# Where the moving operands of split matmuls start in on-chip memory: from 160, 352 and 448 modulo 512 bytes to 64

## The reference

```python
# first block
xn = rms_norm(x, attn_norm_g); proj = xn @ w_in            # 1024 x 3088
y  = concat(moba_attention(...), gated_linear_attention(...) * silu(gr))
x  = x + y @ w_out
hn = rms_norm(x, ffn_norm_g)
h  = causal_dwconv(hn @ w_ffn_up); x = x + (silu(h_gate) * h_val) @ w_ffn_down   # D_FF 2816
x  = rms_norm(x, final_norm_g)
# second block; shifts, scales and gates come from silu(c) @ w_ada + b_ada
x = x + 0.5 * g1 * swiglu(modulate(rmsnorm(x), sh1, sc1), ffn1_w_in, ffn1_w_out)
z = modulate(rmsnorm(x), sh2, sc2) @ w_in_2
y_a = mla_attention(...) @ w_branch_a; y_b = chunk_attention(...) @ w_branch_b
x = x + g2 * ((sigmoid(gate_a) * y_a + sigmoid(gate_b) * y_b) @ w_out_2)
x = x + 0.5 * g3 * swiglu(modulate(rmsnorm(x), sh3, sc3), ffn2_w_in, ffn2_w_out)
return rmsnorm(x, final_norm)
```

## Time and profile before

| | us |
|---|---|
| median of 3 runs | 947.26 |
| lowest, highest | 946.65, 947.27 |
| the profiled execution | 948.89 |
| its span, first to last instruction | 947.2 |
| PE busy in it | 913.0 |
| DVE busy | 698.1 |
| ACT busy | 461.8 |

### The profile page before, as it was taken

How to read it: one execution, slowest core, us unless ns; L and a number is a source line. 1 busy time by engine, 2 the same in 40 slices (tenths; PEclk the granted TensorE clock), 3 DMA queues, 4 the chain that set the end, 5 groups by cost and what they waited for, 6 DMA issues and landing times.

```text
span 947.2 us, 19952 instructions
## 1 busy us (share of the span) xinstructions
PE 913.0 (96%) x7412; PEld 873.5 (92%) x7412; DVE 698.1 (74%) x1080; ACT 461.8 (49%) x698; POOL 64.9 (7%) x109
## 2 busy tenths in 40 slices
PE   7999999999999999999998989999999999999996
PEld 5989898999999988999998979888899899999995
DVE  6498866988889958988889877667757665566444
ACT  4655555755553436433342445656544643444332
POOL 1021101000002210100002121000000000000000
PEclk9999999999999999999999999999999999999998
DMA  7443346556658973988879945543455265655641
GB/s 248 134 143 126 113 144 212 178 179 194 187 193 323 409 287 115 341 286 276 282 253 347 410 175 171 167 153 116 130 173 190 86 201 195 191 186 178 213 142 45
DMA packets 53325, 191.57 MB, mean 202 GB/s; under 512 B 5921, under 2 KB 6433, under 8 KB 53153
## 3 DMA queue, kind: packets, MB, share of 16 engines
q1 hardware_dynamic: 41760, 149.96, 47.2%
q0 software_dynamic: 10656, 39.33, 11.4%
q10 hardware_dynamic: 864, 1.67, 0.5%
HBM read 189.89 MB, written 1.05 MB: 202 GB/s over the span
## 4 chain that ended last, share of the span: by engine, by line
PE 81%; DVE 10%; DMA 4%; ACT 2%; issue 2%; DVEq 0%; ACTq 0%; SPq 0%; POOLq 0%
PE ps L325 24%; PE ps L326 23%; PE ps L327 23%; DMA raw<-w 3%; DVE w_lo L1074 2%; PE ps L399 2%; DVE rstd L1079 1%; PE ps L388 1%; PE ps L389 1%; PE ps L390 1%; DVE ada_raw L1332 1%; PE ps L414 1%; PE ps L471 1%; ACT w_hi L752 1%; PE ps L445 1%
## 5 line engine op out<-in xcount | busy, mean ns | idle before, releaser
L325 PE MATMUL ps<-xh,w_hi 128*128 128x256 f32 x1472 | 416.5, 283 | 11.8 <-DVE xl L1100 10.0
L326 PE MATMUL ps<-xl,w_hi 128*128 128x256 f32 x1472 | 412.8, 280 | 0.0
L327 PE MATMUL ps<-xh,w_lo 128*128 128x256 f32 x1472 | 412.3, 280 | 0.0
L1074 DVE TENSOR_TENSOR w_lo<-raw,w_hi 128x1024 fp32r<-128x1024 f32 x282 | 339.9, 1225 | 97.3 <-ACT w_hi L752 96.9
L752 ACT ACTIVATE w_hi<-raw 128x1024 fp32r<-128x1024 f32 x282 | 288.8, 1056 | 132.6 <-PE ps L327 72.8
L325 PEld LDWEIGHTS ps<-xh,w_hi 128*128 128x128 f32 x1472 | 278.1, 189 | 18.4 <-issue 10.4
L326 PEld LDWEIGHTS ps<-xl,w_hi 128*128 128x128 f32 x1472 | 278.2, 189 | 0.4 <-issue 0.2
L327 PEld LDWEIGHTS ps<-xh,w_lo 128*128 128x128 f32 x1472 | 278.2, 189 | 0.0
L325 PE MATMUL ps<-act_hi,w_hi 128*128 (+1 forms) x528 | 150.4, 285 | 6.1 <-DVE w_lo L1074 6.1
L326 PE MATMUL ps<-act_lo,w_hi 128*128 (+1 forms) x528 | 149.0, 282 | 0.0
L327 PE MATMUL ps<-act_hi,w_lo 128*128 (+1 forms) x528 | 148.9, 282 | 0.0
(11 more groups left out here) (237 smaller groups left out, 926.4 us busy)
## 6 DMA issues: line engine op xcount, KB each, us to landing
raw<-w SPq DMA_DIRECT2D x282, 512.0 KB, 4.3
ada_raw<-ada_w POOLq DMA_DIRECT2D x72, 512.0 KB, 7.2
X<-x_in SPq DMA_DIRECT2D x4, 256.0 KB, 6.5
bm<-bias_in POOLq DMA_DIRECT2D x1, 1024.0 KB, 5.1
out<-X SPq DMA_DIRECT2D x4, 256.0 KB, 2.1
tab<-tab_in ACTq DMA_DIRECT2D x1, 640.0 KB, 9.1
gmask<-gmask_in ACTq DMA_DIRECT2D x1, 512.0 KB, 11.1
cact<-c_in POOLq DMA_DIRECT2D x1, 512.0 KB, 4.8
```

Source lines behind the costliest of these rows:

```text
L325: pe.matmul(o, lh, rh, start=start, stop=False, skip_group_check=True)
L326: pe.matmul(o, lh, rl, start=False, stop=False, skip_group_check=True)
L327: return pe.matmul(o, ll, rh, start=False, stop=stop, skip_group_check=True)
L1074: v.tensor_tensor(w_lo[:, slot(h), :], raw[:, slot(h), :], w_hi[:, slot(h), :].bitcast(F32), ALU.subtract).then_inc(lo_ready, 1)
```

## The change

Three pads change. `off_line`, ahead of xh and xl, grows from 32 to 448 bytes. `on_line`, behind them, grows from 32 to 352 bytes. A new tensor `line2` of 416 bytes stands in the second block's set, between st2 and bm; nothing reads or writes it.

```diff
-        sb("off_line", [P, 8])
+        sb("off_line", [P, 112])
         xh = sb("xh", [P, KC, S], F32R)
         xl = sb("xl", [P, KC, S], F32R)
-        sb("on_line", [P, 8])
+        sb("on_line", [P, 88])
...
-                    ("sm2", [P, 2, 768], F32), ("pt2", [P, 2, 768], F32), ("st2", [P, 2, 3, 4], F32),
+                    ("sm2", [P, 2, 768], F32), ("pt2", [P, 2, 768], F32), ("st2", [P, 2, 3, 4], F32), ("line2", [P, 104], F32),
                     ("bm", [P, 8, S], F32), ("th", [P, 16, S], F32)],
                    early=[("lat", [P, 3, S], F32), ("latsq", [P, 3, S], F32), ("cqh", [P, 3, S], F32R), ("cql", [P, 3, S], F32R)])
```

## The result

The changed kernel takes a median of 941.08 us against 947.26 before. The ratio of its fast runs to those of before is 0.9889, with a 95% interval of 0.9855 to 0.9923. So it is faster, but by 1.1%, and by 0.65% between the medians, where 2.2% was forecast (926.0). Its four runs are 947.24, 930.32, 939.25 and 942.90 us, a spread of 16.9 us, while before has 946.65 to 948.63 here, and 945.48 to 951.06 over 25 runs in the batch of the first experiments. The program and its instructions are the same in each of them. That spread is the first thing to explain.

The account below looks back on a forecast made before the run. PE's distance between matmul starts, set by tile placement, bounds the kernel. Savings of 27.1 us less losses of 2.6, 1.7 and 1.2 leave 21.6; 948.9 less 21.6, less 1.6 to the median, gives 925.7, stated as 926.0; range 920 to 951.

Parts of the forecast that it names:

- What bounds the kernel: Whole kernel: PE, busy 96% of the span; distance between matmul starts, 113.3 to 118.3 ns, goes with tile placement.
- I take 113.3: All split matmuls: every distance falls to 113.3 ns, the cheapest row, from 36 latent-query matmuls (cqh at 448).
- the 27.1 us: Sum of PE savings over all split matmuls at 113.3 ns, before losses where PE waits for others.
- One number for the result: Whole kernel: a single forecast time of 926.0 us, with full gain given 0.50.
- rival 3: Whole kernel: gain only partial, since one placement can settle in more than one pattern; 930 to 944, middle 936 us; chance 0.18.
- Rival 1: Split matmuls: distance between operands counts and 64 bytes is bad, so xh products slow to 118.3 ns; 953.5 us; chance 0.21.
- Weights moving: 1.4 us: Exchanged form, activations stationary and weights moving: 3 x 96 matmuls save 5.0 ns each, 1.4 us.
- Losses in the down projections: 2.6 and 1.7 us: First and second down projections: PE savings lost to waits on DMA and DVE, 2.6 and 1.7 us.
- from 2.15 to 4 us or more: End of first down projection: PE's wait ahead of L399, for the squares of a sum, grows this much if right.
- the forecast of 21.6: Whole kernel: net gain in us, 27.1 less losses of 2.6, 1.7 and 1.2.
- Products with xh outside the up stages, attention outputs, weights moving: 4.2, 1.9 and 1.4 us: 1248 xh matmuls save 3.3 ns each, 3 x 128 attention-output and 3 x 96 weights-moving matmuls 5.0 ns each.
- The rules of the Trainium skill: 16-byte on-chip lines mean the change does nothing; the issue-gap formula gives a 109.2 ns floor, 27 us more PE saving.

Follow-up runs that it names:

- the first experiments: Batch of follow-up runs in which the kernel before, unchanged, also ran 25 times: 945.48 to 951.06 us.
- the sweep: Stand-alone kernel computing nothing of the reference: weights at 128, moving tiles at sixteen multiples of 32 modulo 512, six series of 36 matmuls each; 113.33 to 120.00 ns.
- the best kernel: The changed kernel with w_lo moved by 128 bytes to 256 modulo 512, xh and later moving tiles kept in place: 932.24 us, ratio 0.9831.
- the four exchanged sets: Stand-alone kernel, eight series per set, activations stationary and weights moving: weights at 128, 128 or 128, 0, activations at 64 or 160; 117.0 to 118.75 ns.

## Why the prediction was right and wrong

The sign was right and the size was not. Step by step:

- **What bounds the kernel.** Right: PE's distance between starts, set by placement. DVE's durations did not move (1222 and 1220 ns for 1225 and 1219).
- **"I take 113.3, because after the change both operands of every split matmul start on a multiple of 64."** This is the step that failed. It took one product of 48 matmuls as the value of a kind of placement. That product has this value where it stands, but it is one of two: at 448 the sweep shows 117.8 six times in six, and so does the product itself behind another one. And the reason drawn from it is wrong twice. Weights at 96 with moving at 160, both off a multiple of 64, reach 113.33 once; and of sets with both on it, moving at 64 stays at 117.8 in two series of six with weights at 128, and in eight of eight with weights at 0. What counts is the distance of moving to stationary, modulo 256, together with what stands ahead, the last pause above all. In the profile of after the first output projection and nearly all of the first two down projections are at 113.3, and the three up stages, the second output projection and the last down projection at 117.8. The second value is even above the 116.67 of two stages of before. So the 27.1 us are what a run would save that drew well throughout; the draws made it some 6 to 7 us in the median (941.08 and 940.16).
- **One number for the result.** The text had seen in the earlier trace rows that the same tiles and code give two values, and put that into rival 3 with 0.18. That is the case that came: 936 in the middle there, 941.08 and 940.16 measured, runs from 930 to 947. Had the two values of the earlier trace rows been read as "a placement has a set of values", then one row of cqh would have been a member of such a set, and no floor.
- **Rival 1 (distance, and 64 is a bad one).** The first half is right and the second is wrong: 64 bytes behind is the distance that reached 113.3 most often of all that were measured with w_hi and w_lo alike (11 series of 20). The 953.5 came close for another kernel, the one with w_lo at 256 and nothing else (955.19), where the distances of xh are no good.
- **Weights moving: 1.4 us.** Mostly not gained. In after's profile the stretch of the earlier trace rows shows the forecast 4.76 us for 42, but eight of the ten stretches are at 117.8. In the best kernel it is at 117.6, and in the four exchanged sets at 117.0 to 118.75.
- **Losses in the down projections: 2.6 and 1.7 us.** Too small by about as much again. With all stationary products at 113.33, the two stages should have lost 2.6 and 1.7 of 2.6 us each; they lost 4.1 and 4.0, and so end 1.5 and 1.4 us longer than before. The wait ahead of the sums grew as forecast ("from 2.15 to 4 us or more": 4.19). What was left out is the granted clock behind it, which was at 0.84 in that tail before and fell to 0.76, and in the second from 1.00 to 0.74. By the rows the end waits grew by 2.0 and 0.9 us, the tails by 0.9 and 1.6, and the waits for w_lo ahead of the first halves by 0.8 and 0.5. With this the best kernel's profile gains 14.1 us: 10.6 in the three ups, 2.6 in the last down, 3.8 in head and mixer, less 2.9 in the first two downs. Even with its premise met the forecast of 21.6 would have been too high by 7.5, and by 5.6 when the ratio of 0.9831 is taken (16.0 us), since the profiled execution is one of the longer runs.
- **Products with xh outside the up stages, attention outputs, weights moving: 4.2, 1.9 and 1.4 us.** This is the other half of those 7.5. Head and mixer gained 3.8 us of the 7.5 forecast for them, while the up stages gained what was forecast (11.7 less 1.2; 10.6 measured). Of the missing 3.7 the exchanged form is 1.2; the rest comes of counting every matmul of these short stretches as a gain, and no run here shows where it goes.
- **The rules of the Trainium skill.** In the Trainium skill, SBUF — State Buffer (Specifications (TRN2)) has lines of 16 bytes, by which no multiple of 32 should differ from another. The trace does not agree: sixteen such starts give 113.3 to 120.0 ns. The Trainium skill's TensorE: Matmul & The Clock Gate (Back-to-back issue gap) gives N / 2.4 + 2.5 ns for an isolated matmul, from which 109.2 ns for 256 columns is an estimate; no settled series of split matmuls here is below 113.33.

**What stays open.** What in the chip makes the two patterns, and why distances of 64 and 192 modulo 256 have the good one, no row shows: the weight load of the next matmul starts 2 to 4 ns after the start of the current one in either. Why an fp32 matmul at the pause leads to the good one 29 times in 30 in the kernel, while two series in three behind waits or fp32 matmuls find it in the sweep, is open too. Why the latent queries take the good pattern behind xh at 116.7 and the dear one behind xh at 113.3 is open, and so is what else decides whether the clock falls behind a wait of 2 to 4 us. The exchanged form has no known set that always has 113.3.

## What to carry to other kernels

A matmul's cost is not read from one short product: take the distance between starts over every long stretch, look, in more than one execution, whether it comes in two values, and forecast a spread and not a number where it does. When pads are tuned, treat w_hi, w_lo and the moving tile as one choice and measure it in a small kernel of its own, with several pauses for each placement; here one extra pad of 128 bytes was worth more than the whole change. And before a gain on PE is added up over stages, look where PE already waits for loads: there it comes back as a wait, and with the clock behind the wait it can cost more than it saved.

## What the runs showed of the hardware

- Split matmuls of 256 columns, each with its own weight load, settle at 113.33 to 121.6 ns, by the starts of the operands, nearly modulo 256 bytes; some placements have two settled values, and a stretch keeps its own for over a thousand matmuls (1054 in the second ffn_up of after) until PE pauses.
- A pause of a tenth of a microsecond, with no wait that the profile prints, is enough to change the value (170.74 us in the profile of after).
- With w_hi and w_lo 128 bytes apart modulo 256, and the moving tile 64 below w_hi and 64 above w_lo, all 32 series of three such sets (128, 0 / 64 was measured twice) went to 113.3; in the one shown above it took nine matmuls.
- The granted clock behind the end wait of a down projection: 1.00 after all twelve waits of 1.32 to 1.66 us; after ten of 2.15 to 4.34 us it was 0.73 to 0.85 in nine and 1.00 in one (2.91 us). These are the waits as the rows print them, in the 22 tails of eleven profiles alone, each after a stage in which PE had been busy.
